# Output projection of a gated attention block: from one unit at a time to pairs of units over four PSUM banks

## What is computed

```python
gates = jax.nn.sigmoid(h @ w_gate[l] + b_gate[l]).reshape(B, S, 2, D)
x = x + (gates[:, :, 0] * y_a + gates[:, :, 1] * y_b) @ w_out[l]
hc = rmsnorm(x, norm_cross_g[l])
mem_n = rmsnorm(mem, norm_mem_g[l])
x = x + memory_cross_attention(hc, mem_n, w_xq[l], w_xkv[l], w_xo[l])
```

## Time and profile before

| | us |
|---|---|
| median of 3 runs | 2918.05 |
| lowest and highest | 2917.55, 2918.34 |
| the profiled execution's own time | 2917.15 |
| its span | 2915.4 |
| mean granted TensorE clock, share of full | 0.995 |
| output projection in the trace, first matmul to the next stage's first | 1108.66 to 1287.61 |

### The profile page before, as it was taken

How to read it: one execution, slowest core, us unless ns; L and a number is a source line. 1 busy time by engine, 2 the same in 40 slices (tenths; PEclk the granted TensorE clock), 3 DMA queues, 4 the chain that set the end, 5 groups by cost and what they waited for, 6 DMA issues and landing times.

```text
span 2915.4 us, 35633 instructions
## 1 busy us (share of the span) xinstructions
PE 2859.8 (98%) x13358; PEld 2372.3 (81%) x13358; DVE 1408.8 (48%) x1601; ACT 915.9 (31%) x1165; POOL 127.6 (4%) x121
## 2 busy tenths in 40 slices
PE   7999999999999999999899999999999999999997
PEld 5888888888888887888688888888888888888885
DVE  7666653335873334474544344443434344443436
ACT  5554542224652222243432222222222222222222
POOL 3000000000000003330200000000000000000000
PEclk9999999999999999999999999999999999999998
DMA  4212223222113324233232322222322232232322
GB/s 153 80 65 72 72 77 101 95 93 90 56 58 101 94 98 176 94 104 127 65 101 94 101 94 96 98 94 94 100 96 96 96 100 94 94 101 94 100 94 80
DMA packets 76669, 275.94 MB, mean 95 GB/s; under 512 B 8640, under 2 KB 8768, under 8 KB 76480
## 3 DMA queue, kind: packets, MB, share of 16 engines
q1 hardware_dynamic: 74880, 268.47, 27.7%
q10 hardware_dynamic: 1728, 6.62, 0.6%
HBM read 270.86 MB, written 4.19 MB: 94 GB/s over the span
## 4 chain that ended last, share of the span: by engine, by line
PE 87%; DVE 7%; ACT 4%; issue 1%; ACTq 0%; DMA 0%; DVEq 0%
PE acc L1328 22%; PE acc L1330 22%; PE acc L1329 22%; PE acc L1355 6%; PE acc L1354 6%; PE acc L1353 6%; DVE w_lo L776 1%; ACT pf L424 1%; ACT pf L423 1%; ACT ps L578 1%; DVE act_lo L812 1%; PE ps L1384 1%; ACT w_hi L383 1%; DVE pa_lo L851 0%; ACT sq_sum L565 0%
## 5 line engine op out<-in xcount | busy, mean ns | idle before, releaser
L1328 PE MATMUL acc<-act_hi,w_hi 128*128 128x512 f32 (+1 forms) x2944 | 1143.9, 389 | 22.7 <-DVE act_lo L812 16.1
L1330 PE MATMUL acc<-act_hi,w_lo 128*128 128x512 f32 (+1 forms) x2944 | 1134.5, 385 | 0.0
L1329 PE MATMUL acc<-act_lo,w_hi 128*128 128x512 f32 (+1 forms) x2944 | 1134.2, 385 | 0.0
L776 DVE TENSOR_TENSOR w_lo<-raw,w_hi 128x1024 fp32r<-128x1024 f32 x496 | 628.3, 1271 | 497.6 <-ACT w_hi L383 487.4
L383 ACT ACTIVATE w_hi<-raw 128x1024 fp32r<-128x1024 f32 x496 | 521.3, 1056 | 936.0 <-PE acc L1330 596.9
L1328 PEld LDWEIGHTS acc<-act_hi,w_hi 128*128 128x128 f32 x2944 | 554.5, 188 | 140.8 <-DVE act_lo L812 13.0
L1330 PEld LDWEIGHTS acc<-act_hi,w_lo 128*128 128x128 f32 x2944 | 554.4, 188 | 111.3
L1329 PEld LDWEIGHTS acc<-act_lo,w_hi 128*128 128x128 f32 x2944 | 554.8, 188 | 108.4 <-issue 1.0
L1353 PE MATMUL acc<-act_hi,w_hi 128*128 128x512 f32 x768 | 299.9, 391 | 2.3 <-DVE x L1123 2.3
L1355 PE MATMUL acc<-act_hi,w_lo 128*128 128x512 f32 x768 | 298.8, 389 | 0.0
L1354 PE MATMUL acc<-act_lo,w_hi 128*128 128x512 f32 x768 | 298.8, 389 | 0.0
(11 more groups left out here) (202 smaller groups left out, 1711.7 us busy)
## 6 DMA issues: line engine op xcount, KB each, us to landing
raw<-w_stream SPq DMA_DIRECT2D x496, 512.0 KB, 3.4
x<-x_t SPq DMA_DIRECT2D x8, 512.0 KB, 9.0
x<-x_t ACTq DMA_DIRECT2D x8, 512.0 KB, 8.9
out_t<-x SPq DMA_DIRECT2D x16, 256.0 KB, 2.0
mem<-mem_t ACTq DMA_DIRECT2D x1, 2048.0 KB, 17.7
ra<-pos ACTq DMA_DIRECT2D x1, 256.0 KB, 2.5
par<-params ACTq DMA_DIRECT2D x1, 64.0 KB, 4.0
rc<-rope_const ACTq DMA_DIRECT2D x1, 1.0 KB, 1.7
```

The lines of the kernel that those rows point to most:

```text
L776: nc.vector.tensor_tensor(w_lo[:, s, :], raw[:, s, :], f(w_hi[:, s, :]), ALU.subtract)\
L1328: nc.tensor.matmul(dst, wh, ah, start=start and k == 0, stop=False)
L1329: nc.tensor.matmul(dst, wh, al, start=False, stop=False)
L1330: last = nc.tensor.matmul(dst, wl, ah, start=False, stop=stop and k == UK - 1)
```

## The change

PE takes the 32 units as 16 pairs. A pair opens two banks of four (acc[0], acc[1], the first bank of ps[0], the first bank of ps[1], in rotation). For each block and each of the three products it issues the matmul of the first unit and then that of the second, so successive matmuls go to different banks. Before its first matmul it waits for both units' w_lo and for both banks. The four-bank wait (result n needs result n-4 read) replaces the two-bank one, except for the first two results of the stage, which keep the value of the old wait. DVE reads the bank that belongs to each result. The loads of weights, the matmuls, the conversions and the adds stay the same in number. ACT's, POOL's and SP's programs aren't touched.

```diff
+            def add_of_four(m):
+                n = out_no.n % 4
+                src = acc[n][:] if n < 2 else ps[n - 2][:, 0:S]
+                nc.vector.tensor_tensor(x[:, m, :], x[:, m, :], src, ALU.add).then_inc(acc_free, 1)
+                out_no.add()
...
-                add_out(m)
+                add_of_four(m)
...
-                        add_out(i * 4 + (b + UK * half))
+                        add_of_four(i * 4 + (b + UK * half))
...
+            def bank_of_four():
+                n = out_no.n % 4
+                pe.wait_ge(acc_free, out_no.at(-1 if out_no.n < A_OUT + 2 and not out_no.loops else -3))
+                out_no.add()
+                return acc[n][:] if n < 2 else ps[n - 2][:, 0:S]
+
+            def two_units(tiles, arrive=None):
+
+                pe.wait_ge(lo_done, u.at(2))
+                dst = [bank_of_four() for _ in range(2)]
+                for k, (ah, al) in enumerate(tiles):
+                    if arrive:
+                        pe.wait_ge(*arrive(k))
+                    for m, moving in enumerate((ah, al, ah)):
+                        for n in range(2):
+                            weights = (w_lo if m == 2 else w_hi)[:, (u.n + n) % RING, P * k:P * (k + 1)]
+                            last = nc.tensor.matmul(dst[n], weights, moving, start=k == 0 and m == 0,
+                                                    stop=k == UK - 1 and m == 2)
+                            if k == UK - 1 and m == 2:
+                                last.then_inc(unit_done, 1)
+                u.add(2)
...
-                    for b in range(4):
-                        unit(output()[:], [act_tile(UK * n + k) for k in range(UK)], True, True)
-
-            for b in range(4):
-                unit(output()[:], first, True, True, (lambda k: (mg_lo, k + 1)) if b == 0 else None)
+                    for b in range(2):
+                        two_units([act_tile(UK * n + k) for k in range(UK)])
+
+            two_units(first, lambda k: (mg_lo, k + 1))
+            two_units(first)
```

## The result

| | before, us | after, us |
|---|---|---|
| median of 18 runs each | 2917.95 | 2924.11 |
| lowest and highest | 2916.32, 2920.59 | 2922.44, 2925.02 |
| ratio after to before, 95% interval | | 1.0021 (1.0013 to 1.0028) |
| profiled execution: time, span | 2917.15, 2915.4 | 2922.88, 2921.2 |
| last matmul of the gate stage to last matmul of the kernel | 1789.16 | 1795.28 |

The change costs 6.2 us. On a second chip it cost the same (2923.83 against 2917.70 us). The forecast was +3.3 us, with the range up to 2925.0.

What follows compares the result with a forecast made beforehand. TensorE, busy for 98% of the span, was taken to bound the kernel. Terms 4.09 + 1.49 - 4.87 + 0.72 + 1.85 = +3.3 us on 2918.05 gave 2921.3 us, range 2912.5 to 2925.

Steps and rivals of the forecast that it cites:

- The bound: Output projection: better overlap can bring 4.87 us at most, 0.17% of the time; more needs a shorter matmul.
- The matmul: Distance between the stage's 768 matmuls: stays at 226.67 ns, cost zero, since bank changes between units already cost nothing.
- The rivals of a shorter and of a longer matmul: All 768 matmuls: shorter, 216 ns, 8.4 us saved (chance 0.15); longer, 234 ns, 5.6 us added (chance 0.09).
- The start: Stage's first pair: PE waits for DVE's read of the last gate result, first matmul at 1112.75, +4.09 us.
- The clock behind it: After PE's 3.9 us idle at the stage's start: low clock costs +1.49 us, ends 0 and 3.2 us.
- the old hole: PE's gap near 1119 to 1123 before the change: 3.38 us plus 1.49 us of low clock, both forecast to go.
- Inside the stage: Pairs from unit 16 on: w_lo is ready by 9.2 us, needed at 11.1; cover 1.9 us, no cost.
- The end: Next panel's first matmul waits for a fresh read of acc[0]: +0.72 us, from a 1.17 us wait.
- Behind the stage: Second mem panel: last add ends 3.8 us later, behind a w_lo, delaying the scaling; +1.85 us, ends 0.8 and 2.9.
- The oscillating clock: Rival, whole stage: short idles at bank changes keep dropping the clock to 1.2 GHz; time up to 3075 us, chance 0.01.
- the main case's own range: Whole kernel: 2919 to 2924 us, from the ends of the tail wait and the clock's cost; chance 0.67.
- the prediction's own bound of 0.2%: Whole kernel: smallest effect the measurement can tell from no change, about 0.2%, 5.8 us.

Runs made afterwards that it cites:

- e1: Against the kernel before: four banks in rotation, but one unit at a time, no pairs; 2912.62 us, ratio 0.9982 to before.
- e3: Against the changed kernel: first four and last four units one by one, the 24 between in alternating pairs; 2915.05 us, ratio 0.9988 to before.
- e2: Against the changed kernel: last four units one by one, start unchanged; 2920.05 us, ratio 1.0008 to before.
- e5: Against the changed kernel: in units 16 to 31 DVE and ACT take both results of a pair before converting; 2921.84 us, ratio 1.0016 to before.
- e7: Same kernel as e4, timed on a second chip beside the changed kernel; 2921.56 us, ratio 1.0014 to before.
- e4: Against the changed kernel: 17 unread matmuls to an unused bank while PE waits at the stage's start; 2923.49 us, ratio 1.0015 to before.
- e6: Against the changed kernel: bank rotation shifted by two, so the first pair uses the ps banks nobody reads; 2921.24 us, ratio 1.0009 to before.

## Why the prediction was right

**The bound.** As stated, overlap could bring 4.87 us and no more. e1 brings it: its stage takes 174.08 us, and PE is 4.86 us ahead of the kernel before from there to the idle of 3.24 us in the cross attention. At the end 1789.16 - 1784.55 = 4.61 us are left, since behind that idle the clock was at 0.50 over 5.58 us of PE's busy time in e1 (1398.70 to 1405.50) and over 5.09 us before. In the median it is 5.0.

**The matmul.** Zero was right, and the reason with it: a change of bank was free before. e1 and e3 show it without the ends, 174.08 us both. The rivals of a shorter and of a longer matmul are out. The 8.4 us that the shorter one was priced at also took a float32 matmul of 256 columns for the work of 512 fp32r columns, which no row shows.

**The start.** Right in place, releaser and size (4.31 for 4.09).

**The clock behind it.** This is the term that was mis-sized, by half: 1.49 forecast, 2.98 in the changed kernel's profile and 2.7 in its second one, though 1.5 in e2's and e5's, which have the same wait. I had taken over the price of the old hole from one execution and named 3.2 as the end of the range. Four profiles of the same wait show both sizes, so the right term was something between. The prediction also read from one execution that the clock stays at 1.00 behind an idle of 2.14 us. That idle is in all ten profiles, and in two of them (e2 and the changed kernel's second) the clock fell to 0.50 behind it. A wait of 2 us in the tail should thus have had a clock term too, if a small one.

**Inside the stage.** Right: no pair waited for w_lo.

**The end.** 0.95 for 0.72, from two omissions of 0.1 us each: the matmul came 1.29 us behind unit 30's last one (1289.21 to 1290.50) and not 1.17 as in the earlier trace rows, and the first distance after a wait is longer (0.34 where 0.23 is due).

**Behind the stage.** Right in place and releaser, 2.5 for 1.85. I let w_lo of unit 34 run from 2.7 to 4.5, because POOL would finish beside it. It began at 2.98, since ACT's high part (L641) started 0.26 us behind the add's end (1290.44 to 1290.70), and it took its full 2.25 us. So the last add ended at 5.83 and not at 5.05. Of the 4.6 us by which it moved, 4.5 reached the scaling (16.28 us behind the stage's last matmul before, 20.78 now), and less the slack of 1.0 and PE's own 0.95 they give the 2.5.

**The page's rule.** The Trainium skill's rule of about 216 ns per 512 columns (TensorE: Matmul & The Clock Gate, Back-to-back issue gap) stays in conflict with the trace, 226.7 ns. The oscillating clock that the Trainium skill reports for a kernel that cycles through banks (TensorE: Matmul & The Clock Gate, A second HAM failure mode: psum-queue depth-cycling) didn't come: the clock was 1.00 over 170.48 us of alternation. The page lays it to short idles of PE between groups of matmuls, and here there were none.

The sum was 2.6 us too low against the profiles, 1.5 of it the clock and 0.65 the wait behind the stage. The sign was right. That the time lies in the range is partly luck: 2924.11 is 0.1 us above the main case's own range (2919 to 2924), and the last microsecond up to 2925 had been added for a longer matmul, which didn't come. By the prediction's own bound of 0.2%, a loss of 0.21% with an interval from 0.13 to 0.28% lies on the line between no change and slower.

## What to carry to other kernels

A pair that starts together needs all its banks and all its weights at its start, and leaves two results to be read at its end. Before pairing or interleaving accumulations, look in the rows at what the second one used to wait for under cover of the first, and at who stands between the two reads. More banks in rotation took away a wait that was there; the alternation between them bought nothing, so the two should be tried apart.

## What was not expected of the hardware

The distance of 226.7 ns for 512 fp32r columns doesn't depend on what a matmul shares with the one ahead of it. It is the same when each goes to another bank, when each accumulates in one bank, and for the 17 filling matmuls of e7, which have one weight block, one moving tile, one bank and no accumulation. In its timeline these start at 1108.16, and 16 of them take 3.79 us including the last one's tail of 0.39:

```profile
1107.94 0.39 PE L1336 MATMUL acc<-o_hi,w_lo 128*128 128x512 f32 x1
1108.16 3.79 PE L1608 MATMUL ps<-act_hi,w_hi 128*128 128x512 f32 x16
```

(3.79 - 0.39) / 15 = 0.227 us. What the 13.3 ns over the column time are remains open.

And the same program's times differ by 2.4 to 4.3 us between its 11 or 18 executions, as much as several of the effects studied here. One cause is visible: an equal wait was followed by a low clock that cost 1.5 us in two profiles and 2.7 to 3.0 in two others, and the tail's wait of 2.24 us drew a low clock in one (e7) of the five profiles that have it (the changed kernel's two, e4, e6, e7). The stages ahead of the change do the same: the idle of 2.15 us that ends near 720 was followed by a clock of 0.50 in two of the ten profiles (from 721.85 in e2, from 721.06 in the changed kernel's second, whose stretch is this one):

```profile
721.06:724.47 3.41, 3.41 (x13) 2.93 (x12) 1.44 (x3) 3.33 (x7) 0.00 (x0) 0.50 0.42 119
```

These two executions reach the gate stage's last matmul at 1110.3 us, the others at 1107.9 to 1109.0. So a short wait of PE has no fixed price here. What decides whether the clock falls behind it isn't shown.
